# Four unread identity products in every attention step of the first tile's heads

## What is computed

```python
for l in range(DEPTH):                                   # DEPTH = 2
    mod = c_act @ w_ada[l] + b_ada[l]
    sh1, sc1, g1, sh2, sc2, g2 = jnp.split(mod, 6, axis=-1)
    h = rms_norm(x, norm1_gain[l]) * (1.0 + sc1[:, None]) + sh1[:, None]
    x = x + g1[:, None] * token_mixer(h, ...)            # 6 dilated heads | S5 | 6 latent heads, then w_out
    h = rms_norm(x, norm2_gain[l]) * (1.0 + sc2[:, None]) + sh2[:, None]
    x = x + g2[:, None] * peer_ffn(h, ...)               # top 16 of 16384 experts in each of 8 retrieval heads
```

## Time and profile before

| | us |
|---|---|
| median of 3 runs | 3351.18 |
| lowest and highest run | 3346.34, 3352.05 |
| the profiled execution, its own time | 3348.62 |
| its span, first to last instruction | 3346.8 |
| first gather issued, from the span's start | 228.48 |
| first tile's heads on TensorE | 112.64 to 155.8 |
| first tile's `wo` and `wq` stages | 166.1 to 227.6 |

### The profile page before, as it was taken

The page is one execution under the profiler, slowest core; times in us unless marked ns, Lnnn a source line. Parts: engine busy times, 40 slices in busy tenths (PEclk is TensorE's granted clock), DMA queues, the critical chain, the costliest instruction groups (busy, mean ns, idle before and its releaser), DMA issues.

```text
span 3346.8 us, 45221 instructions
## 1 busy us (share of the span) xinstructions
PE 2372.9 (71%) x15444; PEld 1169.4 (35%) x15444; DVE 2322.8 (69%) x6127; ACT 1452.8 (43%) x4684; POOL 1134.1 (34%) x1028
## 2 busy tenths in 40 slices
PE   8777777677775877767776677766777587775555
PEld 5463334333341433424233233433334143331111
DVE  4269745797568975798357985579756886579554
ACT  2314443345533455344443445334553345434443
POOL 0013333334333334333233333333343333333442
PEclk9688889788987988878888888988998798887777
DMA  7469999999999999999999999999999999999997
GB/s 284 181 229 420 420 420 420 419 402 420 421 419 410 404 420 399 418 416 421 420 421 418 394 421 421 419 419 397 420 420 419 410 403 421 420 419 404 416 421 332
DMA packets 206172, 1336.96 MB, mean 399 GB/s; under 512 B 24350, under 2 KB 38606, under 8 KB 51319
## 3 DMA queue, kind: packets, MB, share of 16 engines
q0 software_dynamic: 147456, 1073.81, 77.7%
q1 hardware_dynamic: 58486, 260.28, 19.6%
HBM read 1325.59 MB, written 10.70 MB: 399 GB/s over the span
## 4 chain that ended last, share of the span: by engine, by line
DMA 44%; PE 23%; DVE 21%; ACT 5%; issue 4%; POOL 3%; SPq 0%; ACTq 0%; POOLq 0%; DVEq 0%
DMA ringbuf<-in_p_uv,IDX 39%; DVE ringbuf L1675 10%; PE PS L889 9%; DMA WB<-in_p_wi 4%; PE PS L669 3%; POOL ringbuf L540 3%; PE PS L856 2%; PE PS L825 2%; ACT v_th L1217 1%; DVE I L1586 1%; ACT DIAG L1229 1%; DVE BC L1586 1%; ACT v_w L1222 1%; PE PS L569 1%; DVE T L1584 1%
## 5 line engine op out<-in xcount | busy, mean ns | idle before, releaser
L540 POOL DMA_INDIRECT ringbuf<-in_p_uv,IDX x1024 | 1133.9, 1107 | 2182.9 <-PE PS L889 1791.1
L889 PE MATMUL PS<-ringbuf,DIAG 64*64 64x512 f32 x8192 | 1286.5, 755 | 803.4 <-ACT DIAG L1229 776.0
L1675 DVE SCALAR_TENSOR_TENSOR ringbuf<-ringbuf,H 128x1024 f32<-128x1024 f32 x1024 | 1234.5, 1221 | 670.6 <-DMA ringbuf<-in_p_uv,IDX 666.6
L889 PEld LDWEIGHTS PS<-ringbuf,DIAG 64*64 64x64 f32 x8192 | 311.0, 158 | 1508.8 <-ACT DIAG L1229 1051.5
L1214 ACT ACTIVATE v_sq<-v_y 128x2 f32<-128x2 f32 x512 | 104.2, 203 | 1450.2 <-DVE ringbuf L1675 1449.6
L1222 ACT ACTIVATE v_w<-v_th,v_g 128x1 f32<-128x1 f32 x1024 | 340.6, 379 | 49.1 <-ACT v_th L1217 1.9
L1217 ACT ACTIVATE v_th<-v_sq,v_y 128x1 f32<-128x1 f32 x1024 | 340.3, 379 | 17.2
L1229 ACT ACTIVATE DIAG<-fold,v_w 128x64 f32<-128x64 f32 x1024 | 300.5, 340 | 18.2 <-PE PS L889 1.6
L856 PEld LDWEIGHTS PS<-HT,WB 128*128 128x128 f32 x1856 | 219.6, 198 | 66.5 <-issue 58.2
L856 PE MATMUL PS<-HT,WB 128*128 128x128 f32 x1856 | 230.4, 284 | 3.1 <-DMA WB<-in_p_wq 3.1
L669 PE MATMUL PS<-WB,HT 128*128 128x256 f32 (+2 forms) x816 | 181.3, 379 | 41.9 <-DMA WB<-in_p_wi 41.9
(11 more groups left out here) (275 smaller groups left out, 2250.1 us busy)
## 6 DMA issues: line engine op xcount, KB each, us to landing
WB<-in_p_wq SPq DMA_DIRECT2D x58, 1024.0 KB, 12.2
WB<-in_p_wi SPq DMA_DIRECT2D x37, 1024.0 KB, 10.3
WB<-in_p_ada SPq DMA_DIRECT2D x36, 1024.0 KB, 10.3
WB<-in_p_wo SPq DMA_DIRECT2D x30, 1024.0 KB, 9.3
ringbuf<-in_p_uv,IDX POOLq DMA_INDIRECT x1024, 18.5
WF<-in_p_ada SPq DMA_DIRECT2D x12, 1024.0 KB, 10.4
WB<-in_p_wi SPq DMA_DIRECT2D x14, 768.0 KB, 8.7
SKT<-in_p_sk SPq DMA_DIRECT2D x64, 128.0 KB, 8.0
```

Source lines behind the costliest of these rows:

```text
L540: pool.indirect_dma_start(out=ring[n % RING], out_offset=None, in_=table, in_offset=bass.IndirectOffsetOnAxis(ap=IDX[:, k % 2, s:s + 1], a ...
L889: mm = pe.matmul(PS[half:half + HALF, 2 * c + r, :], DIAG[r * HALF:(r + 1) * HALF, (n + q) % DIAGS, :], row[r * HALF:(r + 1) * HALF, D + c ...
L1675: dve.scalar_tensor_tensor(row, row, GELU_T, H2[:, k % 2, :], ALU.mult, ALU.mult, accum_out=Y[:, b, q:q + 1]).then_inc(dotted, 1)
```

## The change

A helper issues products of the identity with the constants `CPK`, 440 columns wide, into bank 2. Each writes over what stood there (`start=True`), nothing reads it, and it waits for no semaphore and signals none. In the first tile (`j == 0`) two are issued before `weigh` and two after it in each of the 14 steps of the heads, 56 in all.

```diff
+                def idle_products(count):
+                    for _ in range(count):
+                        pe.matmul(PS[:, 2, 0:CPW], eye, CPK[:, :], start=True, stop=True)
+
@@ the heads' loop: for i in range(2 * HEADS + 2) @@
                         ada_dot(more[i - 1])
+                    if j == 0:
+                        idle_products(2)
                     if 1 <= i <= 2 * HEADS:
                         weigh(i - 1)
+                    if j == 0:
+                        idle_products(2)
                     if i == 2:
                         pe.wait_ge(s5_gate, j + 1)
```

## The result

The changed kernel takes 3368.3 us (median of 4 runs, 3364.6 to 3371.28) against 3348.76 us before (4 runs, 3344.06 to 3352.05): a ratio of 1.0057, 95% interval 1.0044 to 1.0071. It is slower by 19.5 us.

A forecast was written before the change was run, and what follows sets the result against it. TensorE's dense part of the first tile was taken to bound the kernel up to the first gather; heads +20.2 us (21.9 + 41.5 instead of 43.2), behind them -0.5: 3351.2 + 19.7 = 3370.9 us, range 3361 to 3386.

The forecast's parts named there:

- The first gather waits for TensorE, and a delay there is passed on whole: First gather, at 228.48 us, waits for tile 0's last `wq` product; each microsecond before it stands one for one in the total.
- Own work and remaining waits at 2.4 GHz, 21.9 us: Heads: TensorE's work of 19.5 us plus 2.35 us of remaining waits, instead of 43.2 us; a gain of 21.3 us.
- A product costs 0.741 us, all on the path: Heads: price of a 440 column product, scaled by width from `wo`; 56 add 41.5 us, none hidden.
- the 384 column products: Another measure of a product's price: 0.67 us each, by width 0.77 us for 440 columns.
- The waits that go: Heads: of TensorE's 6.2 us of waits, 3.9 us were counted as gone.
- The wait for VectorE's `G`: Start of the heads: a 1.8 us TensorE wait, to be filled by the four products of step 0.
- The bias rows: First chunk in the heads: the third head's rows land near 122.3 us, before they are due at some 125.5, costing nothing.
- The clock is held: Heads: the products keep TensorE at 2.4 GHz, a granted clock near 1.0 where it was 0.54.
- the rival of its loss: Heads: the clock does not stay up; +25 to +50 us for a short relapse, +79 us if it never rises; chance 11%.
- Behind the heads, -0.5 us: Last chunk to `wo`: chunk ends sooner, clock falls in the wait, `wo` starts cold; 0.5 us taken of 3.2 possible.
- The even: Heads: a record costs no more than one of 256 columns, a product 0.431 us, the stage +2.8 us; chance 4%.
- the faster one: Heads: a product passes in one short 0.216 us record, the stage -9.2 us, -12.4 us with the clock held into `wo`; chance 3%.

The follow-up runs named there:

- e2_step0: The changed kernel with only the four wide products of step 0 kept; heads 45.0 us, ratio 1.0012 to the kernel before.
- e10_rows_step0: The kernel before with one weight chunk loaded behind all heads' bias rows, plus four wide products in step 0; heads 30.8 us, ratio 0.9982.
- e3_narrow: The changed kernel with its 56 products 128 columns wide instead of 440; heads 42.4 us, ratio 1.0005 to the kernel before.
- e12_gaps: e11_rows_thin plus five wide products in the wait behind the heads and two in front of `wo`; 3337.19 us, ratio 0.9968 to the kernel before.
- e11_rows_thin: e10_rows_step0 plus one 128 column product on each side of the transpose in the other 13 steps; heads 32.8 us, ratio 0.9978 to the kernel before.
- e9_rows: The kernel before with one weight chunk loaded behind the bias rows of all heads, no products; heads 41.9 us, ratio 0.9992.
- e6_bm_step0: The kernel before with four weight chunks loaded behind the third head's bias rows, plus four wide products in step 0; heads 41.2 us, ratio 1.0011.
- e7_bm_thin: e6_bm_step0 plus one 128 column product on each side of the transpose in the other steps; heads 44.4 us, ratio 1.0006 to the kernel before.
- e1_half: The changed kernel with one wide product on each side of the transpose instead of two, 28 in all; heads 44.4 us, ratio 1.0011 to the kernel before.
- e4_double: The changed kernel with four wide products on each side of the transpose, 112 in all; heads 106.1 us, one run, 3415.18 us.

## Why the prediction was right

It said 3370.9 us, +19.7 us, range 3361 to 3386; measured 3368.3 us, +19.5 us. The mechanism is the predicted one. That the two differences agree to 0.2 us is partly luck: the runs of one kernel lie 7 us apart, and some terms are off by 1 to 2 us and cancel. Step by step:

- **The first gather waits for TensorE, and a delay there is passed on whole.** Shown. With 28, 56 and 112 products it is issued at 229.8, 247.7 and 294.0 us, and from there to the end it is 3118.5, 3115.1 and 3119.4 us.
- **Own work and remaining waits at 2.4 GHz, 21.9 us.** 1.4 us too low: the line through the three runs leaves 23.3 us. The waits are right (five of 0.47 us); halving all of the work was too generous. Most of the excess shows in the two timelines. The first two rows are of the kernel before, the other three of the changed one:

```profile
123.66 0.79 PE L749 MATMUL PS<-KTS,QTS 64*128 64x128 f32 x2
124.39 0.47 PE L757 MATMUL PS<-CPK,PB 128*128 128x128 f32 x1
...
119.49 0.48 PE L753 MATMUL PS<-KTS,QTS 64*128 64x128 f32 x2
119.91 1.74 PE L725 MATMUL PS<-CPK 128*128 128x440 f32 x4
121.49 0.27 PE L761 MATMUL PS<-CPK,PB 128*128 128x128 f32 x1
```

  The logits of the first six heads (64 x 128) take 0.42 us from start to start, where half of 0.73 is 0.37, and the four records behind them take 1.58 us instead of 1.48. That is about 0.15 us a head, 0.9 us in six. L569 takes 1.00 us, not half of 1.86, 0.35 us more in five chunks. What small gains and losses make up the rest stays open.
- **A product costs 0.741 us, all on the path.** 0.725 and 0.739 us by the slopes, 0.37 us a record. The width scaled from `wo` was right; the 384 column products were 4% too dear as a measure.
- **The waits that go.** The wait for VectorE's `G` is gone. The bias rows were priced as hidden, and they were, but I took that for a side remark. With less filling it decided: in e2_step0, which I expected to be faster than before, the clock was lost in that wait, and with the load moved (e10_rows_step0) it held. In e3_narrow the fall stands at the same wait.
- **The clock is held.** Shown: 1.00 over the whole heads, where the rival of its loss had 11%.
- **Behind the heads, -0.5 us.** -1.1 us in the one profile, with the fall where it was placed (4.21 us of idle, L557 1.22 us). e12_gaps holds it to the end of `wo` and is 2.7 us shorter there than e11_rows_thin, of the 3.2 us that the prediction gave as the most; against e9_rows, where it had come back by itself, it is 0.9 us.
- **The rivals.** The even and the faster one both needed a record to cost 0.216 us or less whatever its width; it costs 0.37. The Trainium skill's figure for a stream ("TensorE: Matmul & The Clock Gate", "Back-to-back issue gap", about 131 ns for 512 columns) is not borne out here: the records of 440 columns start every 370 ns. The section names no type for that figure; these products are float32.

The cancellations in the profiled execution: the stage came out 1.3 us longer than predicted (64.7 against 63.4), the stretch behind it 0.6 us shorter (71.6 against 72.2), and the start, where the prediction had no term, 1.3 us shorter, so that the first gather moved by 19.2 us.

## What to carry to other kernels

Work that only keeps TensorE's clock up must cost less than the clock gives, and both are rows of the profile: here 56 x 0.74 = 41 us against 20 us, of which the clock is some 16; at 28 products the two are even. Look for the place where the clock is lost, and fill that alone: four products ahead of the fall were worth more than 56 spread over the stage, once the one transfer that starved TensorE later was out of the way. Products in a wait cost nothing; in front of work that is due they cost their whole length.

## What was unexpected in the hardware

- The heads' own light work held 2.4 GHz for 30 us once four wide products stood at their start (e10_rows_step0), and the same work stayed at 1.2 GHz for 39 us once the clock had fallen at 116 us (e9_rows: L569 1.94 us in every chunk). In these two traces the light work kept whichever level it had. It is no rule: in e6_bm_step0 and e7_bm_thin the clock came back in the middle, some 10 to 13 us after the long wait.
- The clock fell inside a wait of 3.69 us (e2_step0) and at the end of one of 2.14 us (e3_narrow), but also behind waits of 0.89 and 0.20 us in light work (e10_rows_step0), while 0.61 and 0.47 us in the pairs of steps before them did not cost it.
- Ahead of the heads TensorE idles 8.0 us, and the chunk behind that ran at 1.2 GHz in every trace; the clock came back by the end of that chunk or only some 8 us later, behind the next chunk and the transposes (e1_half, e3_narrow, e4_double). So the heads began anywhere between 111.1 and 114.6 us in kernels whose TensorE queue is the same up to there. These 3.5 us are about as large as the differences among half of these kernels, and it is why their heads are compared by length and not by when they end.
